# Running sums and the spatial bias as high and low rows in single-pass products, in a two-layer streaming encoder

## The chip, the cores and the metric

The kernel runs on one core of one Trainium2 chip. The metric is the device time of one launch in microseconds (us), as the median of several runs. The core has five engines that work side by side and meet at semaphores: TensorE (PE, with its weight loads as PEld), VectorE (DVE), ScalarE (ACT), GpSimd (POOL) and SyncE (SP), which only starts transfers. Each engine works through its own instructions strictly in their order.

## The reference

One inference step of an encoder of two layers, for 512 prompt positions and 32 sample positions together (544 columns). Layer 0 mixes by a chunked gMLP gate and a Mamba-2 SSD scan, layer 1 by retention; after each comes a convolution FFN and an embedding gate. The change touches two pieces of layer 0:

```python
def gmlp_mix(u, v, v_gain, w_s, b_s):            # 8 groups, chunks of 128 positions
    u = jax.nn.gelu(u)
    v = rmsnorm(jax.nn.gelu(v)...)
    s = jnp.einsum('gij,bcjgd->bcigd', w, vc) + b_s[:, :n].T[None, None, :, :, None]
    return u * s.reshape(bsz, length, GM_DIM), ...

def ssd_scan(x, dt, a, bm, cm, h0):              # 16 heads
    da = dt * a
    cs = jnp.cumsum(da, axis=2)
    seg = cs[:, :, :, None] - cs[:, :, None, :]
    lmat = jnp.exp(jnp.where(tril, seg, -jnp.inf))
    y_diag = jnp.einsum('bctsg,bctsgr,bcsgrp->bctgrp', cb, lmat, xs)
    ...
```

`b_s` is the spatial bias: one value per group and position, the same for all 128 channels. `seg[t, s]` needs the running sum `cs` once as a column per position and once as a row that stands on every partition.

## The kernel before

**Products.** Large products are made in three passes: a weight slab `w_raw` (1024 columns, transferred into a ring of four slots) is rounded by ACT to `w_hi` (type fp32r), and GpSimd makes `w_lo` = `w_raw` - `w_hi` (L414). Operands are split likewise into `op_hi` and `op_lo`. A `slab` is 48 such products of 256 or 288 columns (L318). Products within layer 0's gate and scan are plain fp32: in a trace each of them shows as two records. The kernel is written by engine, in the order in which each is to work; nothing reorders it later.

**The gate.** Phases come in the order v (8 slabs), u (8), xbc (12), outa, z, outb. After slab u4 (`U_FIRST` = 4) and each of the next seven slabs (u5 to u7, xbc0 to xbc3) TensorE runs `spatial(g)` (L1001): for each of four chunks a product of `ones` with the bias rows `bs_pad` (row 0 is the bias, the others are zero) and one of `v_tok` with `w_spatial` into the same 128 columns of PSUM; the sample's 32 columns get a pair of their own. After spatial 0 comes `cs_sums` (L1017), three products that make the running sums and totals of `da` in bank 2 of `Q`. VectorE makes `da` in `dt_softplus` (L1481), a chain of some twenty small steps that each wait for the one before, and copies the sums in `dt_sums` (L1500). `ya_out` takes a gate's result.

**The scan.** It has five chunks: p = 0 for the sample (32 rows), then p = 1 to 4 of 128 prompt positions. TensorE turns the inputs (L1073, L1078), ACT copies them (`x_copied`), and for each block b of four heads `rows_of_cs(b)` (L1083) puts the running sum as rows on all partitions: four products of a broadcast column of `da` with the triangle `tri`. VectorE's `segments(b)` (L1606) subtracts the column and masks, ACT takes the exponential, VectorE's `mixed(b)` (L1616) multiplies with the scores; `diagonal(b)` multiplies with the inputs `xs`. `rows_of_cs(1)` waits for `x_copied`, b = 2 and 3 wait for the segments of block b - 2; `segments(2)` waits for `diagonal(0)`. Between these TensorE does pieces of the output projection (`between`, L318): 1, 1, 5, 2 and 2 pieces, where one piece is six large products. On GpSimd a chunk is two products: L560 (`y_tok`, after `x_copied`) and L566 (`xsd`, after VectorE's L1594, `xs`), and then `low_ahead` (L414) for the next weights.

## Time and profile before

| | us |
|---|---|
| median of 3 runs | 1858.17 |
| lowest and highest | 1857.85, 1858.92 |
| the profiled execution | 1858.24 |
| its span | 1856.5 |
| granted TensorE clock, mean over the span | 0.991 of full speed |
| TensorE, VectorE, ACT, GpSimd busy | 1816.7, 955.9, 622.5, 847.5 |

The span runs from the first instruction to the last; what lies around it is 1.7 us. Times of rows count from the span's start. A row of the timeline is a start, a length, an engine, a line, what is written and read, and a count of merged records; the length of a product on TensorE includes its way through the array, so starts are to be compared rather than lengths. In brackets stands the idle time of the engine before it and what released it.

### The profile page before, as it was taken

How to read it: one execution, taken by the hardware profiler on the slowest of the kernel's cores; microseconds unless marked ns; L12 is line 12 of the kernel's file. 1: busy time of each engine (PE TensorE's matmuls, PEld its weight loads, DVE VectorE, ACT ScalarE, POOL GpSimd, SP SyncE). 2: the span in 40 equal slices, each digit the busy share in tenths (PEclk: the TensorE clock that was granted, in tenths of full speed). 3: DMA queues.
4: the chain of work that ended last, by engine and by line, in shares of the span. 5: the costliest groups of instructions: out<-in, count | busy, mean ns of one | idle time of the engine just before them, and what ended most of it. 6: DMA issues, size and time to landing. Idle time of an engine off the chain costs nothing.

```text
span 1856.5 us, 34451 instructions
## 1 busy us (share of the span) xinstructions
PE 1816.7 (98%) x14145; PEld 1768.9 (95%) x14145; DVE 955.9 (51%) x1547; ACT 622.5 (34%) x896; POOL 847.5 (46%) x415
## 2 busy tenths in 40 slices
PE   8999999999999999999899999999999999999996
PEld 7999988999999999999899999999899999999995
DVE  6456777565533542556644441344555415515554
ACT  5334423343221222244433332233334313212342
POOL 4333423466544544565533334333365545544662
PEclk9999999999999999999999999999999999999998
DMA  6222201222342232223222222222122222222221
GB/s 231 79 73 69 80 23 35 74 86 80 114 138 89 81 103 90 74 79 98 80 77 77 77 76 80 88 77 78 54 91 82 89 90 90 91 92 82 66 93 48
DMA packets 49475, 156.80 MB, mean 84 GB/s; under 512 B 5984, under 2 KB 10208, under 8 KB 49376
## 3 DMA queue, kind: packets, MB, share of 16 engines
q1 hardware_dynamic: 43776, 147.67, 24.4%
q10 hardware_dynamic: 5600, 7.74, 1.3%
q8 instruction: 71, 1.16, 0.3%
q14 instruction: 28, 0.23, 0.0%
HBM read 149.75 MB, written 5.63 MB: 84 GB/s over the span
## 4 chain that ended last, share of the span: by engine, by line
PE 90%; DVE 6%; ACT 2%; issue 1%; POOL 0%; DMA 0%; DVEq 0%; POOLq 0%; ACTq 0%
PE proj L318 81%; PE Q L925 6%; DVE arena L1753 1%; ACT arena L622 1%; DVE op_lo L389 1%; DVE arena L1616 0%; DVE arena L1606 0%; ACT op_hi L376 0%; PE Q L1202 0%; DVE rstd L369 0%; DVE x L1755 0%; DVE ssq L1426 0%; PE proj L925 0%; DVE arena L1393 0%; PE Q L329 0%
## 5 line engine op out<-in xcount | busy, mean ns | idle before, releaser
L414 POOL TENSOR_TENSOR w_lo<-w_raw,w_hi 128x1024 fp32r<-128x1024 f32 (+2 forms) x276 | 652.3, 2364 | 760.0 <-ACT w_hi L340 759.7
L318 PE MATMUL proj<-op_hi,w_hi 128*128 128x256 f32 (+1 forms) x4272 | 895.6, 291 | 9.5 <-DVE op_lo L389 5.7
L318 PE MATMUL proj<-op_hi,w_lo 128*128 128x256 f32 (+1 forms) x4272 | 884.6, 288 | 0.0
L318 PE MATMUL proj<-op_lo,w_hi 128*128 128x256 f32 (+1 forms) x4272 | 877.8, 287 | 0.0
L318 PEld LDWEIGHTS proj<-op_hi,w_hi 128*128 128x128 f32 x4272 | 683.5, 189 | 22.6 <-issue 12.3
L318 PEld LDWEIGHTS proj<-op_lo,w_hi 128*128 128x128 f32 x4272 | 686.3, 189 | 0.0
L318 PEld LDWEIGHTS proj<-op_hi,w_lo 128*128 128x128 f32 x4272 | 682.0, 188 | 0.0
L340 ACT ACTIVATE w_hi<-w_raw 128x1024 fp32r<-128x1024 f32 (+2 forms) x276 | 284.8, 1032 | 651.0 <-PE proj L318 650.0
L1393 DVE TENSOR_TENSOR arena<-proj,rstd 128x512 f32<-128x512 f32 (+1 forms) x143 | 98.7, 690 | 220.9 <-PE proj L318 195.4
L1400 DVE TENSOR_TENSOR x<-proj,x 128x512 f32<-128x512 f32 x72 | 49.7, 690 | 223.2 <-PE proj L318 223.2
L622 ACT ACTIVATE arena<-arena 128x32 f32<-128x32 f32 (+5 forms) x217 | 106.0, 514 | 54.6 <-DVE arena L1606 33.2
L604 POOL TENSOR_TENSOR arena<-arena,rstd 128x544 f32<-128x544 f32 x44 | 60.0, 1363 | 140.6 <-ACT arena L622 140.6
L405 POOL TENSOR_TENSOR ssq<-ssq,sq 128x544 f32<-128x544 f32 x56 | 90.3, 1613 | 67.7 <-ACT sq L384 67.7
L925 PE MATMUL Q<-arena 128*128 128x256 f32 (+9 forms) x524 | 104.7, 344 | 1.3 <-DVE arena L1616 0.8
L1709 DVE SCALAR_TENSOR_TENSOR arena<-arena,vec 128x546 f32<-128x546 f32 x88 | 96.4, 1095 | 12.4 <-DVE arena L1709 0.3
L925 PEld LDWEIGHTS Q<-arena 128*128 128x128 f32 (+3 forms) x524 | 71.9, 178 | 25.6 <-issue 16.2
L1717 DVE TENSOR_TENSOR arena<-proj,arena 128x512 f32<-128x512 f32 x44 | 30.4, 692 | 120.0 <-POOL arena L604 120.0
L389 DVE SCALAR_TENSOR_TENSOR op_lo<-x,vec,op_hi 128x544 fp32r<-128x544 f32 x48 | 72.1, 1514 | 37.0 <-ACT op_hi L376 33.5
L1707 DVE TENSOR_SCALAR arena<-arena,vec 128x546 f32<-128x546 f32 x44 | 78.2, 1777 | 8.3 <-DVE arena L1697 8.3
L622 ACT ACTIVATE ffn_tail<-arena 128x4 f32 (+1 forms) x44 | 9.1, 206 | 200.0 <-DVE arena L1709 200.0
L1720 DVE TENSOR_TENSOR op_lo<-arena,op_hi 128x544 f32 (+1 forms) x44 | 47.5, 1080 | 40.3 <-ACT op_hi L622 40.3
L622 ACT ACTIVATE op_hi<-arena 128x544 f32 (+2 forms) x46 | 31.0, 678 | 67.5 <-DVE arena L1718 67.5
(171 smaller groups left out, 1040.2 us busy)
## 6 DMA issues: line engine op xcount, KB each, us to landing
w_raw<-in_w_gu SPq DMA_DIRECT2D x88, 512.0 KB, 3.4
w_raw<-in_w_down SPq DMA_DIRECT2D x32, 512.0 KB, 3.4
w_raw<-in_w_heads_a SPq DMA_DIRECT2D x30, 512.0 KB, 3.4
w_raw<-in_w_heads_b SPq DMA_DIRECT2D x18, 512.0 KB, 3.4
w_raw<-in_w_gate SPq DMA_DIRECT2D x16, 512.0 KB, 3.4
w_raw<-in_w_xbc SPq DMA_DIRECT2D x12, 512.0 KB, 3.3
w_raw<-in_w_down SPq DMA_DIRECT2D x16, 384.0 KB, 3.0
w_raw<-in_w_v SPq DMA_DIRECT2D x8, 512.0 KB, 8.2
```

The source lines that it names most:

```text
L318: last = nc.tensor.matmul(proj[:, 2 * g.mod(2) + half, 0:size], w[:, lo:lo + P], o[:, at:at + size], start=(k == 0 and j == 0), stop=(k == ...
L340: nc.scalar.activation(w_hi[:, c:c + width], w_raw[:, c:c + width], ACT.Copy).then_inc(w_hi_done, 1)
L389: nc.vector.scalar_tensor_tensor(out=part(op_lo[ops], n, 0, T), in0=src, scalar=col(gain, n), in1=part(op_hi[ops], n, 0, T), op0=ALU.mult, ...
L405: nc.gpsimd.tensor_tensor(ssq[:, :], ssq[:, :], sq[:, q * T:(q + 1) * T], ALU.add)\
L414: nc.gpsimd.tensor_tensor(w_lo[:, c:c + width], w_raw[:, c:c + width], w_hi[:, c:c + width], ALU.subtract).then_inc(w_lo_done, 1)
L604: nc.gpsimd.tensor_tensor(fsgr[:, q * T:(q + 1) * T], fsg[:, q * T:(q + 1) * T], rstd[:, :], mul).then_inc(sem("f_scaled"), 1)
L622: ins = nc.scalar.activation(dst, src, f, **kw)
L925: return nc.tensor.matmul(out, w, o, start=start, stop=stop)
L1393: a = tt(two(dst(0, TP)), out_prompt(g, rows), two(by[0:rows, f_at:f_at + TP]), mul)
L1400: tt(two(part(x, n, 0, TP)), out_prompt(g), two(part(x, n, 0, TP)), add)
L1707: ins = nc.vector.tensor_scalar(acc, src, w, col(f"fb{layer}", t + -layer * FT), mul, add)
L1709: ins = stt(out=acc, in0=src, scalar=w, in1=acc, op0=mul, op1=add)
```

## The change

**The bias.** `bias_r` (fp32r, 64 rows) holds in row 0 the rounded bias (ACT) and in row 32 what rounding left (`bias_lo`, VectorE, on rows 32 to 63). `spatial` starts with one product of `ones_r` and `bias_r` over 512 columns, then the four of `v_tok`.

**The running sums.** VectorE copies `da` three times side by side (`da_3`), so that five more products in `cs_sums` put 48 rows (three times 16 heads) of running sums along the positions in `Q`. ACT rounds them to `cs_t`, VectorE turns rows 32 to 47 into the rest (`cs_split`). For each chunk GpSimd's `by_block` spreads the rows of each head to the column block of its place among four, by the 0/1 table `pick`, into `cs_b`. `rows_of_cs(b)` is then one single-pass product with the 0/1 column `pick_r` of block b, over 512 columns (128 in p = 0).

The new buffers lie over old ones (`ssq`, `sq`, `w_dt`, `gain_rows`), so a few waits are added for these; one more constant is loaded.

```diff
--- before.py
+++ after.py
...
@@ -182,10 +185,16 @@
         a_row = sb("a_row", SH)
         conv_state = sb("conv_state", XBC * 3)
         conv_tail = sb("conv_tail", XBC * 6)
+        w_dt_at = nc.sbuf_base
         w_dt = sb("w_dt", 8 * SH)
         w_dt_hi = sb("w_dt_hi", 8 * SH, R)
         w_dt_lo = sb("w_dt_lo", 8 * SH, R)
+        pick = sb("pick", 8)
+        pick_r = sb("pick_r", 4, R)
         rstd_root = sq[:, 0:T]
+        cs_t = nc.alloc_sbuf_tensor_at("cs_t", [P, T], R, offset=ssq_at)
+        cs_b = nc.alloc_sbuf_tensor_at("cs_b", [P, 2 * 512], R, offset=sq_at)
+        ones_r = nc.alloc_sbuf_tensor_at("ones_r", [P, P], R, offset=w_dt_at)
 
         class Region:
 
@@ -206,7 +215,9 @@
         r = Region(V_OVER)
         v_buf = r.take(2 * T)
         v_sq = r.take(2 * VT)
+        bias_r = nc.alloc_sbuf_tensor_at("bias_r", [P, D], R, offset=arena_at + 4 * r.at)
         gain_rows = r.take(D)
+        da_3 = arena[:, r.at:r.at + 3 * NP_]
         p_a, p_b, p_c = (r.take(NP_) for _ in range(3))
         assert r.at <= V_OVER + XBC * T
         temps = V_OVER + XBC * T
...
@@ -550,6 +562,21 @@
             phase("xbc")
             low_ahead(pool, PH["outa"], At(0))
 
+            def by_block(p, rows):
+
+                c = NC if p == 0 else p - 1
+                if p >= 2:
+                    pool.wait_ge(sem("cs_rows"), 4 * (p - 1))
+                out = cs_b[0:HL, (p % 2) * 512:(p % 2) * 512 + 4 * rows].rearrange("p (j t) -> p j t", j=4)
+                nc.gpsimd.tensor_tensor(out, cs_t[0:HL, c * CH:c * CH + rows].unsqueeze(1).broadcast_to([HL, 4, rows]),
+                                        pick[0:HL, 0:4].unsqueeze(2).broadcast_to([HL, 4, rows]), mul)\
+                    .then_inc(sem("by_block"), 1)
+
+            pool.wait_ge(sem("cs_split"), 1)
+            pool.wait_ge(consts_in, 16 * N_CONSTS)
+            pool.wait_ge(sem("gm_lo"), GROUPS)
+            by_block(0, TS)
+
             def chunk(p, rows):
 
                 pool.wait_ge(sem("x_copied"), 3 * p + 3)
@@ -566,11 +593,14 @@
                 nc.gpsimd.tensor_tensor(three(xsd, SH), three(xs, SH),
                                         dte[0:rows, c * SH:(c + 1) * SH].unsqueeze(2).broadcast_to([rows, SH, SP_]),
                                         mul).then_inc(sem("xsd_done"), 1)
+                if p < NC:
+                    by_block(p + 1, CH)
 
             for p in range(NC + 1):
                 chunk(p, TS if p == 0 else CH)
                 for n in SSD_MIXED[p] + SSD_END[p]:
                     low_ahead(pool, PH["outa"], At(n))
+            pool.wait_ge(sem("by_block"), NC + 1)
             pool_squares(pool, "n_yb", "n_in")
             phase("z", lambda n: pool_square(pool, "n_yb", n))
             pool_squares(pool, "n_ffn0", "n_yb")
@@ -695,6 +725,19 @@
                     run(p_a, dt_b, ACT.Abs, "dt_abs")
                     act.wait_ge(sem("dt_abs"), 1)
                     run(p_b, p_a, ACT.Exp, "dt_exp", scale=-1.0)
+                if n == 2:
+                    act.wait_ge(sem("gm_in"), 32)
+                    act.wait_ge(sem("v_gained"), GROUPS)
+                    run(bias_r[0:64, :], bs_pad[0:64, :], ACT.Copy, "bias_hi")
+                    act.wait_ge(sem("wdt_lo"), 1)
+                    run(ones_r[0:64, :], ones[0:64, :], ACT.Copy, "ones_set")
+                    run(pick_r[0:HL, :], pick[0:HL, 4:8], ACT.Copy, "ones_set")
+                if n == U_FIRST:
+                    act.wait_ge(sem("cs_mm"), 1)
+                    act.wait_ge(sem("gm_vn"), GROUPS)
+                    run(cs_t[0:HL, 0:TP], Q[0:HL, 3, :], ACT.Copy, "cs_hi")
+                    act.wait_ge(sem("cs_copied"), 1)
+                    run(cs_t[0:HL, TP:T], Q[0:HL, 2, 256:256 + TS], ACT.Copy, "cs_hi")
                 if n == 5:
                     act.wait_ge(sem("cs_copied"), 1)
                     run(ecs, cs, ACT.Exp)
@@ -1004,13 +1047,13 @@
                 if g >= 2:
                     pe.wait_ge(sem("gm_ya"), 2 * g - 2)
                 q = 2 * (g % 2)
-                bias = bs_pad[:, g * P:(g + 1) * P]
+                bias = bias_r[0:64, g * P:(g + 1) * P]
+                mm(Q[:, q, :], ones_r[0:64, :], bias.unsqueeze(1).broadcast_to([64, NC, P]), stop=False)
                 for c in range(NC):
                     at = g * VT + c * P
-                    mm(Q[:, q, c * CH:(c + 1) * CH], ones[:, :], bias, stop=False)
                     mm(Q[:, q, c * CH:(c + 1) * CH], v_tok[:, at:at + P], w_spatial[:, g * P:(g + 1) * P], start=False,
-                       stop=True)
-                mm(Q[:, q + 1, 0:TS], ones[:, :], bias[:, 0:TS], stop=False)
+                       stop=(c == NC - 1))
+                mm(Q[:, q + 1, 0:TS], ones_r[0:64, :], bias[:, 0:TS], stop=False)
                 mm(Q[:, q + 1, 0:TS], v_tok[:, g * VT + TP:(g + 1) * VT], w_spatial[:, g * P:g * P + TS],
                    start=False).then_inc(sem("gm_s"), 1)
 
@@ -1018,7 +1061,12 @@
                 pe.wait_ge(sem("da_done"), 1)
                 mm(Q[:, 2, 0:NP_], tri[:, :], da)
                 mm(Q[:, 2, 128:128 + NC * SH], ones[:, :], da[:, 0:NC * SH])
-                mm(Q[:, 2, 128 + NC * SH:128 + NP_], ones[0:TS, :], da[0:TS, NC * SH:NP_]).then_inc(sem("cs_mm"), 1)
+                mm(Q[:, 2, 128 + NC * SH:128 + NP_], ones[0:TS, :], da[0:TS, NC * SH:NP_])
+                for c in range(NC + 1):
+                    rows = CH if c < NC else TS
+                    out = Q[0:HL, 3, c * CH:(c + 1) * CH] if c < NC else Q[0:HL, 2, 256:256 + TS]
+                    last = mm(out, da_3[0:rows, c * HL:(c + 1) * HL], tri[0:rows, 0:rows])
+                last.then_inc(sem("cs_mm"), 1)
 
             for n in range(KD):
                 slab(pe, PH["u"], At(n), 0)
@@ -1035,10 +1083,12 @@
                     last.then_inc(sem("dt_turned"), 1)
 
                 if n == U_FIRST:
+                    pe.wait_ge(sem("bias_lo"), 1)
+                    pe.wait_ge(sem("ones_set"), 2)
                     pe.wait_ge(sem("gm_mask"), 1)
                     pe.wait_ge(sem("v_padded"), 2)
                 if n == U_FIRST + 1:
-                    pe.wait_ge(sem("cs_copied"), 1)
+                    pe.wait_ge(sem("cs_split"), 1)
                 if n >= U_FIRST:
                     spatial(n - U_FIRST)
                 if n == U_FIRST:
@@ -1086,12 +1136,11 @@
                         pe.wait_ge(sem("x_copied"), 3 * p + 3)
                     elif b >= 2:
                         pe.wait_ge(sem("seg_done"), 16 * p + 4 * (b - 1))
-                    bank = 3 - b % 2
-                    for j in range(4):
-                        h = hc + 4 * b + j
-                        last = mm(Q[0:rows, bank, j * P:j * P + rows], da[0:rows, h:h + 1].broadcast_to([rows, rows]),
-                                  tri[0:rows, 0:rows])
-                    last.then_inc(sem("cs_rows"), 1)
+                    if b == 0:
+                        pe.wait_ge(sem("by_block"), p + 1)
+                    at = (p % 2) * 512
+                    mm(Q[0:rows, 3 - b % 2, 0:4 * rows], pick_r[0:HL, b:b + 1].broadcast_to([HL, rows]),
+                       cs_b[0:HL, at:at + 4 * rows]).then_inc(sem("cs_rows"), 1)
 
                 def diagonal(b):
 
@@ -1494,6 +1543,8 @@
                 link(nc.vector.tensor_scalar(dt_b, dt_b, 0.0, None, ALU.max))
                 link(stt(out=dt_b, in0=p_a, scalar=2.0, in1=dt_b, op0=mul, op1=add))
                 link(stt(out=by_head(da), in0=by_head(dt_b), scalar=-1.0, in1=spread(a_row[:, :]), op0=mul, op1=mul))
+                link(nc.vector.tensor_copy(da_3.rearrange("p (c r h) -> p c r h", r=3, h=SH),
+                                           by_head(da).unsqueeze(2).broadcast_to([P, NC + 1, 3, SH])))
                 nc.vector.memset(da[32:64, n_:], 0.0)
                 nc.vector.memset(da[64:128, n_:], 0.0).then_inc(sem("da_done"), 1)
 
@@ -1502,6 +1553,11 @@
                 link(nc.vector.tensor_copy(cs, Q[:, 2, 0:NP_]))
                 nc.vector.tensor_copy(etot, Q[:, 2, 128:128 + NP_])
                 tt(dte, Q[:, 2, 128:128 + NP_], cs, sub).then_inc(sem("cs_copied"), 1)
+                lo = slice(2 * SH, HL)
+                dve.wait_ge(sem("cs_hi"), 1)
+                tt(cs_t[lo, 0:TP], Q[lo, 3, :], cs_t[lo, 0:TP], sub)
+                dve.wait_ge(sem("cs_hi"), 2)
+                tt(cs_t[lo, TP:T], Q[lo, 2, 256:256 + TS], cs_t[lo, TP:T], sub).then_inc(sem("cs_split"), 1)
 
             def v_scale(g):
                 at, c0 = g * VT, g * (NC + 1)
@@ -1544,6 +1600,8 @@
                 elif n == 2:
                     dt_softplus()
                     nc.vector.memset(s_prompt, 0.0).then_inc(sem("s_zero"), 1)
+                    dve.wait_ge(sem("bias_hi"), 1)
+                    tt(bias_r[32:64, :], bs_pad[32:64, :], bias_r[32:64, :], sub).then_inc(sem("bias_lo"), 1)
                 for g in V_SCALED.get(n, ()):
                     v_scale(g)
                 if n >= U_FIRST:
@@ -1603,7 +1661,7 @@
                     for j in range(4):
                         h = c * SH + 4 * b + j
                         at = (b % 2) * 512 + j * P
-                        stt(out=mix[0:rows, at:at + rows], in0=Q[0:rows, 3 - b % 2, j * P:j * P + rows],
+                        stt(out=mix[0:rows, at:at + rows], in0=Q[0:rows, 3 - b % 2, j * rows:(j + 1) * rows],
                             scalar=cs[0:rows, h:h + 1], in1=neg[0:rows, 0:rows], op0=sub, op1=ALU.min)\
                             .then_inc(sem("seg_done"), 1)
 
@@ -1849,7 +1907,11 @@
     arrays["ffn_state"] = a["state_ffn_conv"][:, 0].reshape(2, 2, FT, P).transpose(3, 0, 2, 1).reshape(P, -1)
     arrays["gain_rows"] = np.broadcast_to(a["gm_v_gain"][None], (P, D))
     arrays["w_spatial"] = a["gm_w_s"].transpose(2, 0, 1).reshape(P, -1)
-    arrays["bs_pad"] = np.concatenate([a["gm_b_s"].reshape(1, -1), np.zeros((P - 1, D), f32)])
+    arrays["bs_pad"] = np.zeros((P, D), f32)
+    arrays["bs_pad"][0] = arrays["bs_pad"][32] = a["gm_b_s"].reshape(-1)
+    row, four = np.arange(P)[:, None], np.arange(4)[None, :]
+    used = (row < SH) | ((row >= 2 * SH) & (row < 3 * SH))
+    arrays["pick"] = np.concatenate([used & (row % 4 == four), used & (row % SH // 4 == four)], 1).astype(f32)
     arrays["ssm_state"] = a["state_ssm"][0].reshape(SH * SP_, SN).T
     arrays["ret_state"] = a["state_ret"][0]
     arrays = {n: np.ascontiguousarray(v) for n, v in arrays.items()}
```

How the instructions stand, at the places of which the next sections speak. TensorE before, from spatial 0 to the first product of slab u5 (names: written <- read; `arena` holds `bs_pad`, `w_spatial` and `da`):

```order
L925 MATMUL Q<-arena,ones 128x128
L925 MATMUL Q<-arena,v_tok 128x128
L925 MATMUL Q<-arena,ones 128x32
L925 MATMUL Q<-arena,v_tok 128x32
L925 MATMUL Q<-arena,tri 128x80 [waits da_done]
L925 MATMUL Q<-arena,ones 128x64
L925 MATMUL Q<-arena,ones 128x16
L318 MATMUL proj<-op_hi,w_hi 128x256 [waits tile_read,w_lo_done]
```

And after:

```order
L968 MATMUL Q<-bias_r,ones_r 128x512 [waits v_padded,gm_mask,gm_vn,ones_set,bias_lo]
L968 MATMUL Q<-arena,v_tok 128x128 x4
L968 MATMUL Q<-bias_r,ones_r 128x32
L968 MATMUL Q<-arena,v_tok 128x32
L968 MATMUL Q<-arena,tri 128x80 [waits da_done]
L968 MATMUL Q<-arena,ones 128x64
L968 MATMUL Q<-arena,ones 128x16
L968 MATMUL Q<-tri,arena 48x128 x4
L968 MATMUL Q<-tri,arena 48x32
L329 MATMUL proj<-op_hi,w_hi 128x256 [waits tile_read,w_lo_done]
```

The four bias products and the sample's have become one wide and one short one that wait for `bias_lo` and `ones_set` besides; five products of 48 rows stand ahead of slab u5.

VectorE after, from the end of `dt_softplus` to the evacuation of slab u3 (u_g<-proj); before, the COPY 128x240 and the product into `bias_r` are not there:

```order
L1544 SCALAR_TENSOR_TENSOR arena<-arena 128x80 [waits dt_steps]
L1545 SCALAR_TENSOR_TENSOR arena<-arena,a_row 128x80 [waits dt_steps]
L1546 COPY arena<-arena 128x240 [waits dt_steps]
L1548 MEMSET arena 32x16 [waits dt_steps]
L1549 MEMSET arena 64x16
L1602 MEMSET arena 128x1024
L1604 TENSOR_TENSOR bias_r<-arena,bias_r 32x1024 [waits bias_hi]
L1442 TENSOR_TENSOR u_g<-proj,rstd 128x512 [waits tile_done]
```

The copy stands inside the linked chain, and `bias_lo` ahead of the evacuation of u3.

GpSimd before, in the scan's sample chunk and the first prompt chunk (`cs_t` and `cs_b` are the running sums as rows and by block; `arena` holds `y_tok` and `xsd`):

```order
L414 TENSOR_TENSOR w_lo<-w_raw,w_hi 128x1024 [waits w_hi_done]
L560 TENSOR_TENSOR arena<-arena,head_rows 32x1024 [waits x_copied]
L566 TENSOR_TENSOR arena<-arena 32x1024 [waits xs_done]
L414 TENSOR_TENSOR w_lo<-w_raw,w_hi 128x1024 [waits w_hi_done]
L560 TENSOR_TENSOR arena<-arena,head_rows 128x1024 [waits y_turned,x_copied]
L566 TENSOR_TENSOR arena<-arena 128x1024 [waits st_mm,xs_done]
```

And after:

```order
L425 TENSOR_TENSOR w_lo<-w_raw,w_hi 128x1024 [waits w_hi_done]
L571 TENSOR_TENSOR cs_b<-cs_t,pick 48x128 [waits gm_lo,consts_in,cs_split]
L587 TENSOR_TENSOR arena<-arena,head_rows 32x1024 [waits x_copied]
L593 TENSOR_TENSOR arena<-arena 32x1024 [waits xs_done]
L571 TENSOR_TENSOR cs_b<-cs_t,pick 48x512
L425 TENSOR_TENSOR w_lo<-w_raw,w_hi 128x1024 [waits w_hi_done]
L587 TENSOR_TENSOR arena<-arena,head_rows 128x1024 [waits y_turned,x_copied]
L593 TENSOR_TENSOR arena<-arena 128x1024 [waits st_mm,xs_done]
L571 TENSOR_TENSOR cs_b<-cs_t,pick 48x512 [waits cs_rows]
```

One product into `cs_b` now stands ahead of the sample chunk's first product, and one right behind the second product of each of the chunks p = 0 to 3.

## Rows read from the trace of the kernel before

**Rows 1.** The page, busy time of the engines: share of the span, instructions.

```profile
PE 1816.7 (98%) x14145; PEld 1768.9 (95%) x14145; DVE 955.9 (51%) x1547; ACT 622.5 (34%) x896; POOL 847.5 (46%) x415
```

**Rows 2.** Timeline, TensorE, u4 to u5: start us, us, what [idle before].

```profile
104.84 0.38 PE L925 MATMUL Q<-arena,ones 128*128 128x128 f32 x2
106.99 0.43 PE L925 MATMUL Q<-arena,tri 128*128 128x80 f32 x2
107.88 0.52 PE L318 MATMUL proj<-op_hi,w_hi 128*128 128x256 f32 x2
113.98 0.47 PE L925 MATMUL Q<-arena,ones 128*128 128x128 f32 x2
```

**Rows 3.** Timeline, ACT and VectorE, 99 to 114 us; last, a 128x1024 row.

```profile
99.06 1.06 ACT L340 ACTIVATE w_hi<-w_raw 128x1024 fp32r<-128x1024 f32 x1 [2.95 <-PE proj L318]
104.27 0.91 DVE L1546 MEMSET arena<- 128x1024 f32 x1 [0.28 <-issue]
105.10 0.63 DVE L1393 TENSOR_TENSOR u_g<-proj,rstd 128x512 f32<-128x512 f32 x1
113.67 0.23 DVE L1504 TENSOR_TENSOR arena<-Q,arena 128x80 f32<-128x80 f32 x1
268.70 1.23 DVE L1594 TENSOR_TENSOR arena<-arena 128x1024 f32<-128x1024 f32 x1 [1.77 <-ACT arena L622]
```

**Rows 4.** Timeline of prompt chunk p = 1 up to its third piece.

```profile
245.91 2.01 PE L925 MATMUL Q<-tri,arena 128*128 128x128 f32 x16
247.68 0.50 PE L318 MATMUL proj<-op_hi,w_hi 128*128 128x256 f32 x2
249.34 1.90 POOL L566 TENSOR_TENSOR arena<-arena 128x1024 f32<-128x1024 f32 x1
249.61 2.78 DVE L1616 TENSOR_TENSOR arena<-arena 128x512 f32<-128x512 f32 x2
251.84 2.00 PE L925 MATMUL Q<-arena 128*128 128x64 f32 x16 [0.20 <-DVE arena L1616]
253.65 0.50 PE L318 MATMUL proj<-op_hi,w_hi 128*128 128x256 f32 x2
```

**Rows 5.** Line L1616 by windows: min/median/max ns, first and last start; p = 0, p = 1.

```profile
L1616 DVE TENSOR_TENSOR arena<-arena x2: 708/1344/1979, 226.2 to 226.8; 32x128 f32<-32x128 f32 x2
L1616 DVE TENSOR_TENSOR arena<-arena x1: 2178/2178/2178, 249.6 to 249.6; 128x512 f32<-128x512 f32 x1
```

**Rows 6.** Groups of GpSimd by shape: count | busy us, mean ns | idle before.

```profile
L414 POOL TENSOR_TENSOR w_lo<-w_raw,w_hi 128x512 fp32r<-128x512 f32 x8 | 10.4, 1296 | 9.6 <-ACT w_hi L340 9.6
L546 POOL TENSOR_TENSOR w_dt_lo<-w_dt,w_dt_hi 128x128 fp32r<-128x128 f32 x1 | 0.5, 453 | 0.0
```

**Rows 7.** Timeline of the sample chunk, p = 0.

```profile
222.55 2.43 DVE L1594 TENSOR_TENSOR arena<-arena 32x1024 f32<-32x1024 f32 x1 [1.92 <-ACT arena L622]
223.87 2.87 POOL L560 TENSOR_TENSOR arena<-arena,head_rows 32x1024 f32<-32x1024 f32 x1
224.91 1.34 DVE L1606 SCALAR_TENSOR_TENSOR arena<-Q,arena,neg 32x32 f32<-32x32 f32 x8
```

**Rows 8.** Windows: length; busy (x instructions) of PE, PEld, DVE, ACT, POOL; granted clock.

```profile
8.00:11.00 3.00, 1.80 (x8) 1.14 (x8) 3.00 (x4) 3.00 (x5) 1.07 (x1) 1.00 1.06 414
11.00:12.00 1.00, 0.87 (x4) 0.55 (x3) 1.00 (x3) 1.00 (x3) 0.00 (x0) 0.68 1.07 387
14.00:15.00 1.00, 1.00 (x7) 1.00 (x7) 1.00 (x1) 0.66 (x2) 1.00 (x1) 0.61 1.06 422
223.00:226.00 3.00, 1.55 (x22) 1.28 (x20) 3.00 (x8) 1.40 (x2) 3.00 (x2) 1.00 0.35 106
226.00:227.00 1.00, 0.80 (x13) 0.63 (x10) 1.00 (x4) 0.31 (x1) 1.00 (x2) 0.70 0.51 205
233.00:234.00 1.00, 1.00 (x9) 1.00 (x9) 0.00 (x0) 0.00 (x0) 0.00 (x0) 0.88 0.00 0
292.00:295.00 3.00, 2.19 (x18) 1.97 (x18) 3.00 (x9) 0.63 (x1) 3.00 (x3) 1.00 0.53 175
```

8 lines of the change are left out of this document (6 added, 2 removed).

## The prediction

> **What bounds the kernel now.** Read the busy shares first: TensorE is busy 98% of the span [rows 1], so time can be won only where TensorE itself sets the pace, and is lost wherever something new makes it stop. Then go to the two places that the diff touches, in order of time.
>
> The first is the gMLP gating, eight calls of `spatial`, after slabs u4 to u7 and xbc0 to xbc3. There TensorE runs without a gap: spatial 0 takes 104.84 to 106.99, the sums 106.99 to 107.88, and slab u5 107.88 to 113.98 [rows 2]. VectorE is late, though: it comes out of the softplus chain with the memset at 104.27 and evacuates slab u3 only at 105.10, as its next item [rows 3], when TensorE has u4 done as well.
>
> The second is the SSD part (sample chunk p = 0, prompt chunks p = 1 to 4). In p = 1 the first two `rows_of_cs` take 245.91 to 247.68; a piece of the output projection, two more `rows_of_cs` and a second piece follow, and TensorE then waits for VectorE's L1616 until 251.84 [rows 4]. That L1616 (`mixed(0)`) began at 249.61 and lasted 2.18 us [rows 4, 5]; the second makes up the rest of 2.78, some 0.68 with the overlap. GpSimd's L566 ran from 249.34 to 251.24. So GpSimd and VectorE, not TensorE, set when `diagonal(0)` starts. The other prompt chunks show the same pattern.
>
> **Part 1: the bias.** One 128-column fp32 product costs 1.77/8 = 0.221 us (245.91 to 247.68 [rows 4]). A single-pass product of 272 columns costs 6.10/48 = 0.127, so 512 columns are 0.24. Per group, four bias products of 0.221 and one of 32 columns go (the ten products take 2.15, so it is (2.15 - 8 x 0.221)/2 = 0.19). In come 0.24 and a short one of 0.02 to 0.13 (bounds: its share of columns, and a whole 272-column product); I take 0.08. That is 0.75 less, and I take 0.70, because the first products after an fp32 one stand at 0.50 against about 0.41 [rows 4] and the group now has such a turn inside. Eight groups: -5.6 (bounds -5.2 to -6.1).
>
> **Part 2: what spatial 0 now waits for.** The order shows VectorE making `da_3` (COPY 128x240) and then `bias_lo` (32x1024) ahead of u3's evacuation, and TensorE's first bias product waits for `bias_lo`. On VectorE the copy adds 0.2 to 0.5 (240 columns; by the memset's 0.91 and L1594's 1.23 for 1024 it is 0.2 to 0.3, with the wait of a linked step behind it some 0.2 more; I take 0.45). The memset at 104.27 moves to 104.72 and ends at 105.6; 32x1024 from SBUF takes about what the undisturbed 128x1024 took, 1.23 [rows 3]. `bias_lo` is there at 106.8, where TensorE came at 104.84: +1.95 (bounds +1.5, with a fast copy and no start-up; +2.4, with a slow one). ACT's three new copies (about 1.06 as L340, and twice 0.2) fit into the 2.95 us that it idles before 99.06 [rows 3] and cost nothing; without that cover they would be 1.5 more on this wait. Queued behind `bias_lo` on VectorE are u3 and the `v_scale` calls; u5 needs u3's bank at about 110, when it has been free for 2.5 us.
>
> **Part 3: the sums.** Four products of 128 columns and one of 32 are added in `cs_sums`: 4 x 0.221 + 0.1 = +1.0, on TensorE's path. Slab u5 starts at 107.88 + 1.95 - 0.70 + 1.0 = 110.1 and ends at 116.2. `cs_split` must be there then: dt_sums ended at 113.9 [rows 3], VectorE and GpSimd's L414 shift by about 1.7 to 2, and the two subtractions add 0.8: 116.3. So +0.1 (bounds 0 and +1). Sum of the gating part: -5.6 + 1.95 + 1.0 + 0.1 = -2.55.
>
> **Part 4: the products in prompt chunks.** TensorE's 16 products of 0.221 become four of 0.24, 2.6 us less per chunk. All of it stands before `diagonal(0)`, whose start is set by L566 and L1616. It buys nothing and turns into waiting: 0.
>
> **Part 5: `by_block` behind L566.** The order shows a 48x512 product on GpSimd right behind L566 in p = 0 to 3. Nearest row: 1.30 us for GpSimd's 128x512 into fp32r [rows 6]; I take 1.3 (lower bound 0.9, by half of L566's 1.90 [rows 4]). Who gets in next when both engines want SBUF? In p = 0 two GpSimd products stand back to back while two L1616 are queued: the first L1616 lasts 0.71, the second 1.98 [rows 5], for 32x128 elements, a quarter of the columns that `mixed(1)` in p = 1 does in 0.68. So the two engines alternate: L1616, L566, L1616. In p = 1 to 3 `mixed(0)` gets in as now, `by_block` comes next, and `mixed(1)` behind it: end 251.79 + 1.3 + 0.68 = 253.8. `diagonal(1)` needs it and now starts at about 252.73 (251.84 + 4 x 0.221): +1.05. TensorE-bound pieces follow (253.65 [rows 4]), so this stays: 3 x 1.05 = +3.2 (bounds 0, if `mixed(1)` gets in first, and +3.9). The Trainium skill (SBUF — State Buffer, "Who interferes with whom") says the same of a VectorE instruction with two SBUF inputs against GpSimd: an exclusive lock, the loser blocks wholly. By that rule, the trace agrees.
>
> **Part 6: the sample chunk.** `by_block(0)` stands behind L414 on GpSimd; VectorE's L1594, queued since 222.55, got in first when L414 ended (L560's start, 223.87), and ended at 224.98 (L560 behind it took 2.87 for 1.9); `by_block(0)` (0.45 for 128x128 [rows 6]) ends at 225.4. VectorE's segments start at 225.6 where they started at 224.91 [rows 7]: +0.7. Some comes back, because one product stands for four in each block and `diagonal(0)` also waits for TensorE's own piece here. I take +0.3 (bounds: -0.4, if only the four blocks' shorter products count, some 0.1 each; +0.7).
>
> Sum without any change of clock: 1858.24 - 2.55 + 3.2 + 0.3 = 1859.2.
>
> **Part 7: the clock.** The granted clock was 1.00 (2.4 GHz) and fell to 0.50 (1.2 GHz) shortly after 8:11, where TensorE had 8 matmuls and was busy 1.80 of 3 us, and shortly after 223:226, busy 1.55 of 3. It held through 292:295, busy 2.19. Counting the parts of the mixed rows (0.68 in 11:12 is 0.64 us slow, 0.61 in 14:15 is 0.78, 0.70 in 226:227 is 0.60, 0.88 in 233:234 is 0.24), the first fall lasted 3.4 us, from 11.4 to 14.8, and the second 6.8, from 226.4 to 233.2 [rows 8]. In the new p = 1, from 247.8 to 251.1 TensorE has only two short products and one piece of 0.8 (busy about 1.5 of 3), and from 250.8 to 253.8 only `diagonal(0)` (0.9 of 3): as empty as the stretches before a fall or emptier, and p = 1 to 3 alike. At spatial 0 it is busy 1 of 3 us. Each fall costs half of its slow time where TensorE sets the pace: 1.7 us for a short one, 3.4 for a long one. I expect a fall in two or three of the five places, at 1.7 to 2.5 each: 2.5 x 2.1 = +5.3 (bounds 0; 5 x 3.4 = +17).
>
> The Trainium skill (TensorE: Matmul & The Clock Gate, "Why this matters for your kernels") ties drops of the clock to single idle gaps longer than any that this change makes. By it there would be none of part 7 and the time would be 1859.2. The rows at 223:226 speak against it, since with 1.55 busy of 3 no gap there can be over 1.45 us.
>
> **The forecast: 1859.2 + 5.3 = 1864.5.** The sum is made against the profiled execution's 1858.24 (its span is 1856.5), which is within 0.1 of the median of the runs, 1858.17.
>
> **Rivals.**
> - *The clock holds* (part 7 is nothing): 1859.2, from 1857.5 to 1861. For it: the idle pieces are each under 2 us. It is the page's case too. Chance 0.30.
> - *The port is free*: `mixed(1)` gets in ahead of `by_block`, or `by_block` is short, and the clock mostly holds: 1858.24 - 2.55 + 0.3 = 1856.0, from 1854 to 1858. Against it: the 1.98 us in rows 5. Chance 0.13.
> - *The products are on the path after all*: then 4 x 2.6 us come back in the SSD part and parts 5 and 7 are hidden: 1858.2 - 2.6 - 10.4 = 1845. For it: TensorE is 98% busy. Against it: the wait before 251.84 is on VectorE already. It decides if `mixed(0)` ends earlier with earlier rows. Chance 0.07. Faster.
> - *The clock stays low through the chunks*: a fall in each of four chunks of 3.4: 1873 and above. Chance 0.06.
>
> **How the numbers follow.** The forecast's case (two to four falls; 1861 to 1870) has 0.44. 1855.5 to 1870 holds it, the case of the held clock and most of the free port: 0.8. A run of this kernel can tell 0.2%, 3.7 us, from no change. Faster than 1854.5: the third rival and a tail of the second, 0.10. Slower than 1861.9: most of the forecast's case and the last rival, 0.46. The rest, 0.44.
>
> **What the new profile would show.** Right: TensorE idle some 2 us before the first `bias_r` product, released by VectorE; spatials 1 to 7 shorter by 0.7; TensorE idle about 1 us before each `diagonal(0)`; a second L1616 of about 2 us in p = 1 to 3; the clock at 0.50 in some stretch near p = 1 to 4. Wrong: chunks that are shorter than now, a `by_block` that runs beside L1616, or single-pass products much above 0.24, which would move all of part 1.

## The result and the profile after

The changed kernel takes 1875.83 us (median of 4 runs, 1874.09 to 1879.53), the kernel before 1858.2 (1857.85 to 1858.92, 4 runs): a ratio of 1.0096, 95% interval 1.0083 to 1.0109. It is slower by 17.6 us. The forecast was 1864.5 with a range that ended at 1870, so the direction was right and the size was not. The profiled execution took 1877.49 us, its span is 1875.7, and its mean granted clock 0.981 where it was 0.991.

The page after, busy time of the engines and the granted clock in 40 slices. TensorE has 194 records fewer than in [rows 1] (79 products, since a plain fp32 one shows as two records) and is busy 11 us longer: work was taken away and what is left runs slower.

```profile
PE 1827.8 (97%) x13951; PEld 1768.8 (94%) x13951; DVE 959.8 (51%) x1551; ACT 624.2 (33%) x901; POOL 854.5 (46%) x420
...
PEclk9989987999999999999999999999999999999998
```

The slices are coarse, so the windows come next (length, busy time of PE, PEld, DVE, ACT, POOL, granted clock), at spatial 0 and in the prompt chunk p = 1:

```profile
104.00:107.00 3.00, 1.09 (x6) 0.58 (x5) 2.66 (x4) 0.00 (x0) 0.00 (x0) 0.95 0.30 122
107.00:110.00 3.00, 3.00 (x13) 2.60 (x12) 3.00 (x8) 1.60 (x2) 0.99 (x1) 0.50 0.00 0
...
116.00:119.00 3.00, 3.00 (x23) 3.00 (x22) 0.15 (x2) 0.00 (x0) 0.00 (x0) 0.85 0.00 0
...
257.00:260.00 3.00, 1.94 (x8) 1.16 (x8) 3.00 (x6) 1.26 (x2) 3.00 (x3) 1.00 0.26 105
260.00:263.00 3.00, 2.62 (x13) 2.62 (x13) 2.32 (x5) 0.00 (x0) 1.22 (x1) 0.55 0.00 0
263.00:266.00 3.00, 3.00 (x15) 3.00 (x16) 2.32 (x9) 1.26 (x2) 0.00 (x0) 0.50 0.00 0
266.00:269.00 3.00, 3.00 (x21) 3.00 (x21) 1.47 (x3) 1.06 (x1) 0.03 (x1) 0.81 0.00 0
```

A clock of 0.50 is 1.2 GHz, 1.00 is 2.4. The first stretch lasts from 106.7 to 116.9 us: 10.2 us (0.05 x 6, then 9, then 0.15 x 6). TensorE is busy all the time in it, at half speed. The second lasts 6.8 us. Read in windows of 1 us, the whole run has these slow stretches (without the idle start and end of the kernel): 10.2 us at spatial 0, 13.6 in the sample chunk p = 0 (229.6 to 243.2), 6.8, 10.2 and 10.2 in p = 1, 2 and 3, and 3.4 at 922. That is, before rounding, 54.6 us where before had 17.1 (3.4 at 11 us, 6.8 in p = 0, 6.8 at 902; counts of [rows 8] and one more of that kind).

Where in time does the loss arise? The start of the first transposes of each chunk is a mark that all kernels here have. After:

```profile
227.07 1.05 PE L1123 MATMUL Q<-ident,arena 128*32 128x128 f32 x8 [0.78 <-ACT arena L652]
...
252.91 1.04 PE L1123 MATMUL Q<-ident,arena 128*128 128x128 f32 x8
...
304.86 1.03 PE L1123 MATMUL Q<-ident,arena 128*128 128x128 f32 x8
...
332.16 1.04 PE L1123 MATMUL Q<-ident,arena 128*128 128x128 f32 x8
...
352.07 1.04 PE L1182 MATMUL Q<-ident,arena 128*128 128x128 f32 x8
```

With the mark of p = 2 at 278.61 and the same marks of the other traces this table follows. "Up to p = 0" is the time from the start of the span, it holds the gate; the others are lengths.

| kernel | up to p = 0 | p = 0 | p = 1 | p = 2 | p = 3 | p = 4 |
|---|---|---|---|---|---|---|
| before | 220.57 | 23.81 | 22.57 | 22.29 | 23.37 | 19.91 |
| after | 227.07 | 25.84 | 25.70 | 26.25 | 27.30 | 19.91 |
| difference | +6.50 | +2.03 | +3.13 | +3.96 | +3.93 | 0 |

The differences add up to 19.55 us; the spans differ by 19.2. So everything happens before 352 us, and a third of it in the gate. These are rows of one execution, which was 1.7 us above the median.

What TensorE waited for between 90 and 345 us: us in all, times, longest.

```profile
PE Q L968 <- DVE arena L1664: 4.4, 8, 1.3
PE Q L968 <- POOL cs_b L571: 3.2, 1, 3.2
PE Q L968 <- DVE bias_r L1604: 1.9, 1, 1.9
PE Q L968 <- DVE arena L1674: 1.3, 2, 0.7
```

The largest of these in a prompt chunk is 1.3 us (in p = 3). With two smaller rows that are not shown the waits add up to 12.6 us, in the kernel before to 4.5. The slow stretches are no waits and stand in none of these rows.

### The profile page after: what moved, and what is told of

Its sections match the earlier page's. It is cut to its first block, busy times and chain, and to the rows that moved or that the text cites. A ratio compares the mean times of both kernels' runs of the same rounds, so it can differ in the third digit from the quotient of the medians.

```text
span 1875.7 us, 34083 instructions
## 1 busy us (share of the span) xinstructions
PE 1827.8 (97%) x13951; PEld 1768.8 (94%) x13951; DVE 959.8 (51%) x1551; ACT 624.2 (33%) x901; POOL 854.5 (46%) x420
## 4 chain that ended last, share of the span: by engine, by line
PE 83%; DVE 7%; issue 5%; POOL 2%; ACT 2%; DMA 0%; POOLq 0%; DVEq 0%; ACTq 0%
PE proj L329 75%; PE Q L968 6%; POOL w_lo L425 1%; DVE arena L1811 1%; ACT arena L652 1%; DVE op_lo L400 1%; DVE rstd L380 1%; ACT op_hi L387 0%; DVE ssq L1475 0%; DVE arena L1664 0%; PE Q L1251 0%; DVE arena L1442 0%; DVE x L1813 0%; PE proj L968 0%; DVE arena L1396 0%
## 5 line engine op out<-in xcount | busy, mean ns | idle before, releaser
L968 PE MATMUL Q<-arena 128*128 128x256 f32 (+9 forms) x524 | 109.7, 358 | 1.9 <-DVE arena L1674 1.3
L968 PEld LDWEIGHTS Q<-arena 128*128 128x128 f32 (+3 forms) x524 | 76.7, 191 | 26.3 <-issue 16.2
```

The source lines that it names most:

```text
L968: return nc.tensor.matmul(out, w, o, start=start, stop=stop)
```

## The experiments

The times of all twelve, in us, with the total of slow stretches in the profiled run (start and end of the kernel left out again) and the ratio to the kernel before on the same chip:

| kernel | median | ratio, 95% interval | slow |
|---|---|---|---|
| before | 1858.2 | | 17.1 |
| after | 1875.8 | 1.0096 [1.0083, 1.0109] | 54.6 |
| 1 thin | 1864.3 | 1.0038 [1.0023, 1.0052] | 30.7 |
| 2 fill | 1866.3 | 1.0042 [1.0025, 1.0059] | 10.3 |
| 3 bias | 1861.0 | 1.0013 [1.0004, 1.0023] | 20.5 |
| 4 bias early | 1857.6 | 0.9995 [0.9985, 1.0004] | 17.1 |
| 5 bias, 128 rows | 1852.3 | 0.9970 [0.9957, 0.9983] | 17.1 |
| 6 late by_block | 1874.5 | 1.0084 [1.0066, 1.0102] | 47.8 |
| 7 sums only | 1870.7 | 1.0065 [1.0047, 1.0083] | 44.4 |
| 8 fill p = 0 | 1856.5 | 0.9990 [0.9980, 1.0000] | 10.2 |
| 9 combination | 1850.3 | 0.9960 [0.9946, 0.9974] | 13.7 |
| 10 after, 128 rows | 1865.9 | 1.0048 [1.0033, 1.0064] | 44.4 |
| 11 thin, refilled | 1857.9 | 1.0001 [0.9991, 1.0010] | 13.7 |
| 12 combination, six fillers | 1850.1 | 0.9958 [0.9945, 0.9972] | 6.8 |

**Theory A**: TensorE got emptier at the places of the change, its granted clock fell there, and that is the loss. **Theory B**: the new instructions and waits cost the time, and the clock is a by-product. A second question came up with the first runs: why the bias part gave so little (theories **R** and **D**).

### 1 and 11: the idleness alone

```diff
 def rows_of_cs(b):                     # in the kernel before
     ...
-    for j in range(4):
+    for j in range(1):
         last = mm(Q[0:rows, bank, j * P:j * P + rows], ...)
```

> The kernel before, with nothing of the change in it, but with three of the four head products of each block of the scan left out (all segments of a block read the first head's columns; output not the reference's). It takes the same work off TensorE in the chunks (48 + 12 products of 0.22 us over p = 1 to 4, and less in p = 0) as the change does, without by_block, without the sums, without the bias. Theory A (TensorE's emptiness lowers its granted clock, and that is the +17.6): slow stretches appear in p = 1 to 3 that before has not, 6.8 to 10 us each, half of that lost where TensorE sets the pace: 1858.2 + 10 to 15, so about 1868 to 1873. Theory B (the new instructions and their waits cost the time; the clock is a by-product): 1858 or less, and no new slow stretches. Theory C (the products were on the path after all): about 1848.

Nothing new is in this kernel, there is only less in it, and it is slower by 5.9 us. There are two new slow stretches, 6.8 us each, in p = 1 and p = 3; the one of p = 0, where 12 small products are gone too, is 10.2 for 6.8; the one at 11 us is not there. Windows of the first:

```profile
248.00:251.00 3.00, 1.73 (x12) 1.32 (x11) 3.00 (x9) 1.26 (x2) 3.00 (x2) 1.00 0.51 162
251.00:254.00 3.00, 2.13 (x12) 1.91 (x10) 1.73 (x2) 0.00 (x0) 0.57 (x1) 0.66 0.02 5
```

p = 0 to p = 4 last 24.59, 25.63, 22.30, 26.00 and 19.93 us. In p = 1 and p = 3 that is 3.1 and 2.6 more than before, for a stretch of 6.8 each. In p = 2 the clock held and the chunk took 22.30 for 22.29: taking 2.65 us of work off TensorE gained nothing, which is part 4 of the prediction. Theory C is out. The size was below what I expected (10 to 15), since only two of the three chunks had a fall, and none of 10 us.

Experiment 11 gives the work back as other work:

```diff
     bank = 3 - b % 2
+    if p:
+        for _ in range(3):
+            mm(Q[:, bank, P:4 * P], op_hi[1][:, 0:P], op_hi[1][:, 0:3 * P])
     for j in range(1):
```

> The kernel of the first experiment, where three of the four head products of a block are left out, with three single-pass products of 384 columns of slab data in front of each block's one product in p = 1 to 4 (0.18 us each by 512 columns in 0.24), which give TensorE about the work back that was taken; nothing else differs (output not the reference's, as there). Theory A: the idleness alone brought its slow stretches in p = 1 and p = 3, so they go and the time falls from 1864.3 to 1858 to 1860. If it was something else in that kernel: 1864.

1857.9, the time of before. The same window as above, and the next:

```profile
248.00:251.00 3.00, 2.78 (x17) 2.36 (x16) 3.00 (x7) 1.26 (x2) 2.86 (x2) 1.00 0.30 123
251.00:254.00 3.00, 2.66 (x23) 2.54 (x23) 2.34 (x8) 0.17 (x1) 0.00 (x0) 1.00 0.03 5
```

p = 1 to 4 last 22.55, 22.29, 23.34 and 19.92. The two kernels differ in nothing but the fillers, so in this kernel the falls in the prompt chunks come from TensorE's emptiness. For that part of the change theory A is shown. Emptiness does not decide it alone, though: p = 2 and p = 4 of experiment 1 had an emptiest 3 us as empty as p = 1's (1.72 beside 1.73 us busy), and held.

### 2: the changed kernel, filled

```diff
 if n == U_FIRST:
+    pe.wait_ge(sem("gm_vn"), 1)
+    for _ in range(8):
+        mm(Q[:, 0, :], op_hi[0][:, 0:P], op_hi[0][:, 0:512])
     pe.wait_ge(sem("bias_lo"), 1)
 ...
 rows_of_cs(0)
+keep(1)                # so many products of 512 columns into bank 1
 rows_of_cs(1)
 between(SSD_PIECES[p][0])
+keep(2)
 rows_of_cs(2)
+keep(3)
 rows_of_cs(3)
 between(SSD_PIECES[p][1])
+keep(3)
 diagonal(0)
+keep(3)
 diagonal(1)
```

> The changed kernel with idle time of TensorE filled: 8 single-pass products of 512 columns before spatial 0, and 1, 2, 3, 3 and 3 in the waits of each chunk, into banks that are overwritten afterwards; the result is unchanged. Some of them will lie on the path: each is 0.24 us, and where the fill is longer than the wait it costs the rest, some 0 to 1 us per chunk. Theory A: the clock holds at 1.00 at spatial 0 and in p = 1 to 3, and the time comes back to the sum without the clock, 1859.2, plus up to 4 for fillers on the path: 1859 to 1863. Theory B: no gain, 1876 or more.

The clock held at spatial 0 and in p = 1 to 4; what is left are 3.4 us at 13, 3.4 in p = 0 and 3.4 at 911. The time fell by 9.6 us, though 12 fillers per chunk lay partly on the path: p = 4, which has no by_block and no fall in either kernel, got 1.02 us longer. I had expected 1859 to 1863; the miss is these fillers (about 1 in each of five chunks) and the bias part, which is not the -5.6 of the sum (next). Theory B, no gain, is out. With by_block in place and the clock held, p = 1 to 3 lasted 23.34, 23.29 and 24.07 us, 2.5 in all more than before where the changed kernel had 11.0. That is 0.8 a chunk, and fillers alone cost 1.02 in p = 4.

### 3, 4 and 5: the bias alone, without its wait, and with 128 rows

Experiment 3 is the kernel before with the bias lines of the change. Experiment 4 makes `bias_hi` (ACT) and `bias_lo` (VectorE) at u0 in place of u2. Experiment 5 is 4 with

```diff
-run(bias_r[0:64, :], bs_pad[0:64, :], ACT.Copy, "bias_hi")
+run(bias_r[:, :], bs_pad[:, :], ACT.Copy, "bias_hi")
-run(ones_r[0:64, :], ones[0:64, :], ACT.Copy, "ones_set")
+run(ones_r[:, :], ones[:, :], ACT.Copy, "ones_set")
 ...
-mm(Q[:, q, :], ones_r[0:64, :], bias.unsqueeze(1).broadcast_to([64, NC, P]), stop=False)
+mm(Q[:, q, :], ones_r[:, :], bias.unsqueeze(1).broadcast_to([P, NC, P]), stop=False)
```

and the same for the short product.

> The kernel before with the bias part of the change alone (no sums, no by_block; four-product rows as before). Prediction's part 1 and 2 without da_3's copy: -5.6 + 1.5 = -4.1. Theory A: TensorE's wait before spatial 0 brings a fall of the clock there (in the changed kernel it lasted 10.2 us, half of it lost), and the chunks keep their clock: -4.1 + 5.1 - 1.7 (if the fall at 11 us stays away, as there) to +1: 1857.5 to 1859.2. If the clock held: 1854. Theory B with a single-pass bias dearer than thought: 1858 with the clock held and spatials hardly shorter than 2.15.

> As the one with the bias part alone, but bias_hi on ACT and bias_lo on VectorE are issued two slabs earlier, behind v_sum(7), where VectorE has time, so that spatial 0 finds them ready and TensorE does not wait. Part 1 of the prediction alone: 1858.2 - 5.6 = 1852.6 (1852 to 1853.5), the clock at 1.00 at 105 to 117 us. If the single-pass rows were dearer than 0.24 it would be 1855 or more; if the earlier VectorE work delayed the norms, 1854.

Experiment 3: 1861.0, 2 above the forecast's upper end. TensorE waits 1.48 us for `bias_lo` (1.5 was forecast), and a slow stretch of 6.8 us follows. Experiment 4: no wait, no slow stretch there, and still 1857.6 in place of 1852.6. So 5 us of part 1 do not exist, whatever the clock does. TensorE in one spatial of experiment 4, then its weight loads (PEld), then both in experiment 5; start us, us:

```profile
121.79 0.49 PE L935 MATMUL Q<-bias_r,ones_r 64*128 64x512 f32 x1
122.22 1.16 PE L935 MATMUL Q<-arena,v_tok 128*128 128x128 f32 x8
123.30 0.28 PE L935 MATMUL Q<-bias_r,ones_r 64*128 64x32 f32 x1
123.51 0.41 PE L935 MATMUL Q<-arena,v_tok 128*128 128x32 f32 x2
```

```profile
121.79 0.18 PEld L935 LDWEIGHTS Q<-bias_r,ones_r 64*128 64x128 f32 x1
122.21 0.97 PEld L935 LDWEIGHTS Q<-arena,v_tok 128*128 128x128 f32 x8 [0.24 <-issue]
123.30 0.18 PEld L935 LDWEIGHTS Q<-bias_r,ones_r 64*128 64x128 f32 x1
```

```profile
120.95 0.39 PE L935 MATMUL Q<-bias_r,ones_r 128*128 128x512 f32 x1
121.18 1.05 PE L935 MATMUL Q<-arena,v_tok 128*128 128x128 f32 x8
121.99 0.26 PE L935 MATMUL Q<-bias_r,ones_r 128*128 128x32 f32 x1
122.10 0.39 PE L935 MATMUL Q<-arena,v_tok 128*128 128x32 f32 x2
```

```profile
120.82 0.19 PEld L935 LDWEIGHTS Q<-bias_r,ones_r 128*128 128x128 f32 x1
120.95 1.09 PEld L935 LDWEIGHTS Q<-arena,v_tok 128*128 128x128 f32 x8
121.96 0.19 PEld L935 LDWEIGHTS Q<-bias_r,ones_r 128*128 128x128 f32 x1
```

With 64 rows each load starts with its own product: 121.79 and 121.79, 122.21 and 122.22, 123.30 and 123.30. With 128 rows it starts 0.03 to 0.23 us ahead, under the product before. From start to next start the long product costs 0.43 and 0.23 us, the four of `v_tok` 1.08 and 0.81, the short one 0.21 and 0.11.

> The bias part alone and early, as before, but with ones_r and bias_r of all 128 rows (rows past 64 are zero) where they had 64. The traces so far show that the 512-column product starts only when its weights begin to load (121.79 for both), that the next fp32 product's weights begin to load at its own start too, and that a group took 1.97 us for 2.15; 128-row weights of before begin to load 0.13 us ahead of their product, in the shadow of the one before. Theory R (rows): the lead is lost because the products of 64 rows stand between products of 128 rows. Then with 128 rows a group falls to about 1.5 (0.24 + 4 x 0.22 + 0.1 + 0.2), its period from 8.15 to 7.5 to 7.7, and the time to 1853 to 1854. Theory D (data): each turn between single-pass and fp32 products costs the lead, whatever the rows. Then nothing changes: 1857.6 and a period of 8.15.

1852.3: theory R. The period from group to group is 7.45 us (120.95 to 128.40) where it was 8.15 in experiment 4 and 8.22 before, and the mark of p = 0 stands at 214.46 for 219.41. Two products in each of eight groups, with weights of 64 rows among those with 128, had cost 4.95 us at the mark. (Experiment 5 started spatial 0 0.32 us earlier, 104.29 for 104.61, and had a new wait of 0.59 before its second group, so this is not exactly eight times the 0.70 of the periods.) The Trainium skill (TensorE: Matmul & The Clock Gate, "Step-by-step: what each phase is for") says that a weight load is pulled ahead of the running product when the row groups do not conflict or when it goes to the background weight buffer, and that its time does not depend on the number of rows. For the load's own time the trace agrees, 0.18 us and 0.19. What the load adds to a row of products does depend on the rows here, 0.70 us per group: the load of 64 rows is not pulled ahead, nor the one of 128 behind it. Why the chip holds them back, no run shows.

### 6 and 7: by_block later, and the sums alone

Experiment 6 moves `by_block(p + 1)` on GpSimd from the end of `chunk(p)` to behind the `low_ahead` calls that follow it.

> The changed kernel, but by_block for the next chunk stands behind the chunk's low_ahead (L425 in the profile after) on GpSimd, out of the way of the second L1674. Prediction's part 5, that by_block costs 1.05 us in each of p = 1 to 3 by holding mixed(1): the first pair of L1674 in p = 1 falls from 3.62 back to 2.78 us and each of the three chunks gets 1.0 to 1.3 shorter: 1875.8 - 3.2 = 1872.6 (1870.5 to 1874), the slow stretches as they are or shorter. Theory that part 5 is nothing and the chunks' +11 is all clock: 1875 to 1877.

VectorE's first two L1674 of p = 1 after the change (with GpSimd's by_block, L571, beside them):

```profile
257.88 1.90 POOL L593 TENSOR_TENSOR arena<-arena 128x1024 f32<-128x1024 f32 x1
258.15 3.62 DVE L1674 TENSOR_TENSOR arena<-arena 128x512 f32<-128x512 f32 x2
...
259.74 1.48 POOL L571 TENSOR_TENSOR cs_b<-cs_t,pick 48x512 fp32r<-48x512 f32 x1
...
260.38 3.67 PE L968 MATMUL Q<-arena 128*128 128x64 f32 x16 [0.66 <-DVE arena L1674]
```

They took 2.78 before [rows 4] and 3.62 here; p = 2 and 3 show 3.63 and 3.62, and p = 4, behind which no by_block stands, 2.79. In experiment 6 they take 2.22, 2.79, 1.91 and 2.79. So the second one does wait for by_block: 0.84 us in each of three chunks. Single, the two L1674 of p = 1 are 2.18 (258.15 to 260.33) and 1.52 us; by_block, on record from 259.74, ends at 261.22, 0.89 behind the first of them. That is part 5's mechanism and nearly its size (1.05). But by these rows it cost next to nothing here. `diagonal(0)` is four products of 0.221 us at full clock; at half clock they last until about 262.15 (260.38 + 2 x 0.88), and the second L1674 ended at 261.77. The slow clock covers the collision. The kernel gained 1.3 us (the runs overlap, 1870.85 to 1876.56 beside 1874.09 to 1879.53), and not by this: p = 1 and p = 3 lasted 27.43 and 29.19, longer than after, since by_block now came too late for the next chunk.

```profile
249.28 2.02 POOL L571 TENSOR_TENSOR cs_b<-cs_t,pick 48x512 fp32r<-48x512 f32 x1
...
251.35 0.73 PE L968 MATMUL Q<-cs_b,pick_r 48*128 48x512 f32 x2 [2.48 <-POOL cs_b L571]
```

My edit exchanged a hidden collision for an open wait of 2.48 us, and can't price part 5 by its time. By accident it showed something else. Its work up to p = 0 is that of the changed kernel, and TensorE is as empty before spatial 0, 1.08 of 3 us busy beside 1.09, with waits of 1.92 and 1.91. Windows of experiment 6:

```profile
104.00:107.00 3.00, 1.08 (x7) 0.62 (x5) 2.68 (x3) 0.00 (x0) 0.00 (x0) 1.00 0.34 134
107.00:110.00 3.00, 3.00 (x23) 2.76 (x24) 3.00 (x8) 1.60 (x2) 1.04 (x1) 1.00 0.00 0
```

Here the clock held. The first `bias_r` product starts at 106.47, 0.06 ahead of the changed kernel's, and the mark of p = 0 is at 222.50 and not at 227.07: one fall of 10.2 us cost 4.5 to 4.6 (4.57 between the marks). The same instructions with the same wait had a fall in one execution and none in the other.

> The changed kernel without the bias part: bias products as before, so spatial 0 does not wait, and the sums and single-pass rows as in the changed kernel. Theory A: no fall of the clock at spatial 0; cs_sums +1.0, and from p = 0 on the same +2.1, +3.1, +4.0, +3.9 that the starts of the chunks show in the changed kernel: 1858.2 + 14.1 = 1872.3. If the falls in the chunks depend on the one at 106 us they go too: 1862.

Experiment 7 (the change without its bias lines) is at 1870.7, 1.6 below the forecast. TensorE does not wait at spatial 0, there is no fall, and the mark of p = 0 is at 221.48, +0.91 for the sums (+1.0 forecast). From there on it is like the changed kernel: 24.89, 25.20, 25.98, 27.15 and 19.93. The falls in the chunks don't depend on the one at spatial 0.

### 8, 9 and 12: filling the sample chunk, and the combination

```diff
     between(SSD_PIECES[p][0])
+    if p == 0:
+        pe.wait_ge(sem("x_copied"), 2)
+        for _ in range(4):
+            mm(Q[:, 1, :], op_hi[1][:, 0:P], op_hi[1][:, 0:512])
     rows_of_cs(2)
     rows_of_cs(3)
     between(SSD_PIECES[p][1])
     diagonal(0)
+    if p == 0:                         # experiment 12 alone
+        for _ in range(2):
+            mm(Q[:, 1, :], op_hi[1][:, 0:P], op_hi[1][:, 0:512])
     diagonal(1)
```

> The kernel before with four single-pass products of 512 columns into a bank overwritten later, in the sample chunk, where TensorE waits 1.45 us for VectorE before its third rows (225.67). Theory A: the clock holds at 1.00 through 226.4 to 233.2 and half of these 6.8 us, or what of it TensorE sets, comes back: 1858.2 - 2 to -3.4 = 1855 to 1856. If the fillers do not keep the clock: 1858.2, and if they lie on the path and it falls all the same, 1859.

1856.5, a gain of 1.8 that lies at the edge of what is measured (0.9980 to 1.0000; single runs go from 1855.0 to 1858.1). In the profiled one the fall came later and was shorter, 3.4 us from 229.0, behind a wait of 0.59 us before `diagonal(1)`.

> The two things together that each made the kernel before faster: the bias part early with 128 rows (1852.3) and the four fillers in the sample chunk (-1.8). If they add: 1850.5 (1849.5 to 1851.5), no slow stretch at 220 to 228. If the fall only moves to another place of the chunk or the next: 1852.3.

> As the combination of early 128-row bias and four fillers, with two more fillers between diagonal(0) and diagonal(1) of the sample chunk, where with four fillers alone TensorE still waited 0.59 us for L1620 and a fall of 3.4 us followed. If the clock then holds: another -1 to -1.7 against the combination, 1849 to 1850. If the fall stays, or the two lie on the path: 1850.5 to 1851.

Experiments 9 and 12 stand on experiment 5, so they have the bias part of the change and not the running sums. They compute all that the reference asks for and are the fastest, 1850.3 and 1850.1, both 0.4% faster than before. I can't tell them apart by time, and beside experiment 5 alone (1852.3) the fillers are worth about 2 us. The profiled run of 9 had its fall in p = 0 all the same (6.8 us; that run took 1852.68), the one of 12 had none:

```profile
218.00:221.00 3.00, 2.27 (x24) 1.61 (x23) 3.00 (x11) 0.69 (x3) 3.00 (x2) 1.00 0.54 175
221.00:224.00 3.00, 3.00 (x29) 2.29 (x28) 2.85 (x8) 0.31 (x1) 1.63 (x1) 1.00 0.00 0
```

The five runs of 12 lie within 1849.95 to 1851.5, those of 9 within 1849.59 to 1852.96.

### 10: the changed kernel with the bias mended

The changed kernel with `bias_hi` and `bias_lo` early and 128 rows, as in experiment 5.

> The changed kernel with its bias part early and of 128 rows; sums, by_block and the single-pass rows of the scan as they are. From the changed kernel: -4.7 to -5 for the rows, -1.9 for the wait before spatial 0, and about -5 for the fall there if it stays away: 1875.8 - 12 = 1864 (1862 to 1867), with three to five slow stretches left, all from p = 0 on. If the time there was not the bias's, above 1868.

1865.9, as forecast. The mark of p = 0 is at 215.80, 11.3 us ahead of the changed kernel's. That is near the sum of the wait (1.91), the fall behind it (4.57) and the loads of 64 rows (4.95). By the medians, leaving the bias part out (experiment 7) saves 5.1 of the changed kernel's 17.6 us, and mending it saves 10.0, since the mended part also gains. The chunks are 25.21, 25.30, 26.09, 27.23 and 19.91, again as in the changed kernel: 11.8 us more than before (123.74 against 111.95), with slow stretches of 10.2, 6.8, 10.2 and 10.2 us in p = 0 to 3.

No run has the mended bias and the fillers of experiment 2 together in the changed kernel. An estimate: experiment 2's five chunks took 117.61 us for the 123.74 here, so it would come to about 1865.9 - 6.1 = 1859.8. That is above experiment 5, which leaves the running sums as they were; by this estimate the running-sum part does not pay with these fillers, though they hold the clock.

## Why the prediction was wrong, step by step

- **Part 1, the bias: the term mis-sized, -5.6 forecast, about -1 measured** (experiment 4: 219.41 for 220.57, of which 0.23 had arisen before spatial 0, which starts at 104.61 for 104.84 [rows 2]). The products themselves are nearly as cheap as I said, 0.23 and 0.11 from start to start in experiment 5. What I left out is that weights of 64 rows between weights of 128 are not loaded ahead. With 128 rows the same part gives -6.1 at the mark (214.46), or -5.6 from the start of spatial 0 (104.29), which is the forecast. I had priced the turn between kinds of product with 0.05 per group, by the 0.50 of the first products behind an fp32 one, and had no term for the rows; these cost 0.70 per group.
- **Part 2, the wait at spatial 0: right.** +1.95 forecast; 1.91 in the row of the first `bias_r` product, released by L1604.
- **Part 3, the sums: right.** +1.0 and +0.1; experiment 7 shows +0.91 at the mark, +1.2 from the start of spatial 0 (104.53).
- The gate without the clock was forecast at -2.55. Experiment 6, whose clock held, shows +1.93. The 4.5 us between are part 1.
- **Part 4, no gain from fewer products: right**, by p = 2 of experiment 1 (22.30 for 22.29) and by p = 4 of the changed kernel itself (19.91 for 19.91).
- **Part 5, the collision: right as a mechanism** (0.84 us for 1.05 in each of three chunks, with by_block at 0.89 behind the first L1674 for 1.3, my lower bound), and by the rows hidden in the sum, as it lies beside a `diagonal(0)` at half clock. At full clock no run prices it by itself: in experiment 2 the pair of L1674 took 3.63 us too, but three fillers stand between the two diagonals and cover it. Whether the collision helps to bring the falls is not shown either.
- **Part 6, the sample chunk: the forecast of VectorE was right, that of TensorE was missing.** VectorE's first segment starts 5.05 us behind the mark (232.12 - 227.07) for 4.34 before, +0.71. But TensorE waits 3.19 us for by_block(0), with 0.23 of 3 us busy in 229 to 232, and the slow stretch grows from 6.8 to 13.6 us. The chunk got 2.03 us longer for +0.3. (In experiments 6, 7 and 10, where TensorE has the same instructions in this chunk, the stretch was 10.2 us and the chunk 0.85, 1.08 and 1.40 longer.) `by_block(0)` itself took 1.38 us where I had 0.45, beside VectorE's L1652.
- **Part 7, the clock: the step that failed, in number and length of the falls.** I expected a fall in two or three of five places at 1.7 to 2.5 us each, +5.3. There was one in all five, of 10.2, 13.6, 6.8, 10.2 and 10.2 us. The one at spatial 0 cost 4.57 (after against experiment 6); p = 1 to 3 grew by 3.13, 3.96 and 3.93, where a thinned chunk whose clock held did not grow (p = 2 of experiment 1, p = 4 of the changed kernel). Together with most of p = 0's 2.03 that is about 17. The lengths that I took as bounds (3.4 and 6.8) were the two that the trace of before happened to show; my bound of +17 was right, and yet the range ended at 1870. The rival "the clock stays low through the chunks: 1873 and above" was what happened, with a chance of 0.06.

By the terms, for the profiled execution: forecast were -2.55 for the gate, +0.3, +3.2 and +5.3 for the clock, 6.25 in all. Measured were +1.93 for the gate with the clock held, 4.57 for its fall, 2.03 for p = 0, 11.02 for p = 1 to 3 and -0.35 behind them, 19.2 in all. Of the miss of 12.95 the bias's rows are 4.5 and the clock, with what it hid of part 5 and with part 6, is 8.8 (4.57 + 2.03 + 11.02 - 0.3 - 3.2 - 5.3). The median lies 1.7 below that execution.

The rule that was weighed there (the Trainium skill, TensorE: Matmul & The Clock Gate, "Why this matters for your kernels": drops come from single idle gaps, longer ones than the change was expected to make) does not hold for the prompt chunks. In p = 1 after the change the longest wait of TensorE before the fall was 0.66 us and the clock fell; in experiment 11 the waits were filled and it held. At spatial 0 it fell behind 1.91 us, and behind 1.48 in experiment 3. In p = 0 a wait of 3.19 us arose, but the kernel before fell there with 1.45 as its longest. In the other direction a wait of 1.91 us brought a fall in one execution and one of 1.92 none in another.

What stays open: what decides whether a given stretch brings a fall, and how long it lasts. Here they lasted from 3.4 to 13.6 us. The same emptiness did not always bring one. These are the emptiest 3 us of p = 1 and of p = 4 after the change, in steps of 1 us from the chunk's mark:

```profile
256.91:259.91 3.00, 1.94 (x8) 1.16 (x8) 3.00 (x7) 1.26 (x2) 3.00 (x3) 1.00 0.30 119
336.16:339.16 3.00, 1.95 (x8) 1.17 (x8) 3.00 (x6) 1.26 (x2) 2.60 (x2) 1.00 0.00 0
```

Behind the first the clock fell, behind the second it held. So it went in each of the four profiled kernels that have these chunks and no fillers (after, 6, 7 and 10): a fall in every p = 1 to 3, none in p = 4. Only behind p = 4 stands no by_block; whether that is the reason was not tried. The fall at 11 us, which all kernels could have, was there in some profiled runs and not in others. The spread of the runs fits chance: 5.4 us between the changed kernel's four runs, 1.8 between 20 runs of the kernel before. It was not tried whether the single-pass rows of the scan, whose weights have 48 rows, would gain from 128. Their loads show the same sign: after the change one load starts at 254.54 together with its own product, for which nothing else had to be waited for, and the load of the slab behind another at 258.70, together with its product.

## What to carry over

Work that is taken off an engine while it waits for others anyway buys nothing, and on TensorE it can cost: look at how empty the stretch gets, and price a new stretch that is as empty as one before a fall with a long fall, not with the shortest seen, and remember that it may hold. Where such a stretch can't be avoided, a few products into a bank that is overwritten later are cheap insurance, if they fit into the wait; twelve in a chunk that needed none cost 1.02 us. And when a product with few rows is put among products of 128 rows, give it 128 with zeros: the rows are free, the load that is not hidden is not.

## What the runs showed of the hardware

- Weights of 64 rows between weights of 128 start to load only with their own product, and so do the next ones of 128. Filled up to 128 rows, the period of a group fell from 8.15 to 7.45 us, and eight groups took 4.95 less (219.41 against 214.46).
- Taking 48 products away in the prompt chunks (and 12 small ones in the sample's) made a kernel 5.9 us slower; putting idle work in place of the 48 gave all of it back (1864.3, 1857.9).
- A fall of the clock to 0.50 over 10.2 us of full work cost 4.57 us, near the half.
- A stretch as empty as one before a fall (1.95 beside 1.94 of 3 us busy) had none in four kernels out of four.
- The same instructions behind the same wait (1.91 and 1.92 us) had a fall in one execution and held in another.
- A product of 48x512 on GpSimd took 1.48 us beside VectorE's L1674 and 1.03 elsewhere (experiment 6, at 267.25), and delayed the next L1674 by 0.84: both lost, each by the other. 0.59 of the 1.48 passed before the first L1674 had ended (259.74 to 260.33).
